# Moving the second layer's eight VectorE modulation slots into the first feed-forward, as sixteen half slots

## The chip, the cores and the metric

One Trainium2 chip, one core of it. The metric is the device time of one execution in microseconds (us); the kernel before takes 1564.17 us, the median of three runs.

## What is computed

A first block (a gMLP and RWKV mixer, then a mixture of 32 experts) and a second block of two transformer layers, over 256 tokens of width 1024, all in float32. Only the second block matters here. Cut to that:

```python
def second_block(x, c, w_mod, b_mod, ...):
    c_act = jax.nn.silu(c)                                          # (1, 1024)
    for i in range(2):
        mod = jnp.einsum('bd,dm->bm', c_act, w_mod[i]) + b_mod[i]   # (1, 6144)
        sh_a, sc_a, gt_a, sh_f, sc_f, gt_f = jnp.split(mod, 6, axis=-1)
        h = modulate(rmsnorm(x, g_mix_pre[i]), sh_a, sc_a)
        qkv = jnp.einsum('bsd,de->bse', h, w_qkv[i])
        ...                                                         # attention, 16 heads
        x = x + gt_a[:, None, :] * rmsnorm(o, g_mix_post[i])
        h = modulate(rmsnorm(x, g_ffn_pre[i]), sh_f, sc_f)
        gate = jnp.einsum('bsd,df->bsf', h, w_ffn_gate[i])          # f: 2816
        up = jnp.einsum('bsd,df->bsf', h, w_ffn_up[i])
        gate = causal_depthwise_conv(gate, w_conv[i], b_conv[i])    # width 3
        y = jnp.einsum('bsf,fd->bsd', jax.nn.silu(gate) * up, w_ffn_down[i])
        x = x + gt_f[:, None, :] * rmsnorm(y, g_ffn_post[i])
```

The vector `mod` of layer 1 depends on `c` and `w_mod[1]` alone, so it can be computed at any time before it is used. (Layers are counted from 0 in the code: layer 1 is the second.)

## The kernel before

Each engine runs its own program, and semaphores tie them. SyncE (SP) issues all weight loads on one DMA queue, in program order. Most go to `ring`, six slots of 2 MB, in turn; SP waits on `slot_freed` before it loads into a used slot, and TensorE on `slot{s}_loaded` before it reads one.

**Modulation.** `w_mod` of a layer is 1024 x 6144. Its 6144 columns are three groups of 2048 (group 0: `sh_a`, `sc_a`; group 1: `gt_a`, `sh_f`; group 2: `sc_f`, `gt_f`). A unit is 256 rows of one group, 2 MB, so a group has four units. Units are computed in one of two ways. On TensorE, `mod_slice` multiplies a unit in a ring slot by a column of SiLU(c), `silc`, into bank 0 of PSUM, `part`. On VectorE (DVE), a unit is a slot: `mod_slots` takes its two halves of 128 rows (1 MB each, tiles `mslots` in the arena), multiplies each by one column of `silc` and adds it into `macc2` (line 1892 for the first half of a group, line 1894 for all others), each step giving `mod_step`. TensorE then adds the 128 partitions of `macc2` into `part` with a column of ones (`add_slots`, line 1129). From there ScalarE (ACT) copies `part` to SBUF (`part_copy`), TensorE turns it into columns (`flush`, line 579) and DVE adds the bias into `modc` (`mod_columns`, line 1465).

Layer 1's group 0 is done by TensorE during layer 0. Its groups 1 and 2 are the eight slots of this case. SP loads them between the `w_qkv1` matrices (line 386), two slot buffers in turn, each load waiting for the `mod_step` that frees its buffer; the very first also waits for the end of the layer before (`x4_ready`). DVE works them off during layer 1's projections, and TensorE has `add_slots` and `flush` between projection units: after unit 4 the sum of group 1, after unit 8 the sum of group 2, and flushes after units 5 and 9. Units 0 to 7 are Q and K (line 1164), 8 and 9 are half of V (line 1182); the next work of TensorE is the scores of the attention (lines 1219 and 1220 in layer 0, 1224 in layer 1), which waits for ACT's copies of V (line 2306). `add_slots` waits for the `mod_step` count, and everything of TensorE stands behind it, since an engine runs in order.

**Feed-forward.** 22 tiles of 128 of the 2816 columns, in five ring groups of four tiles and a last one of two. A group is three loads: gate, up and down matrices, 2 MB each (line 430, `ffn_group`). For tile f TensorE runs `gate_up` (32 matmuls, line 1349, into bank 5 + f % 2); DVE runs `conv` (lines 2043, 2046, 2049), ACT the SiLU (line 2383), DVE `gated` (line 2054, gives `act_f`); and TensorE runs `down` of tile f (8 matmuls, line 1362), which waits for `act_f`. The order on TensorE is gate_up(f + 1), down(f), gate_up(f + 2), down(f + 1) and so on:

```python
gate_up(cur, 0, f)
down(prev, 3, f - 1, last_of=(0, 1, 3))     # frees the three slots of the group before
gate_up(cur, 1, f + 1)
down(cur, 0, f)
```

The three loads of group g + 1 wait for slots that group g - 1 frees in down(4g - 1), that is, right behind gate_up(4g).

Of the kernel before, what the change touches and what calls it, by code (L numbers as in the profile page):

```python
# [111 lines left out]
def build_program(nc, a):  # L112
    with ExitStack() as ctx:
# [128 lines left out]
        gmixb, gffnb = at(12288, D), at(13312, D)  # L242
        macc2 = at(10240, 2 * D)
        mslots = ((at(8192, 2 * D), at(12288, 2 * D)), (at(15360, 2 * D), at(17408, 2 * D)))
        diagd = at(14336, DC, P)
        t1 = at(15360, 2, 2, 384)
        sp_ = at(16896, 2, 2, 384)
# [30 lines left out]
        def _(sp):  # L278
# [82 lines left out]
            for layer in range(2):  # L361
                if layer == 0:
                    for i in range(4, 6):
                        load_mod("w_mod0", i)
                def qkv(i):

                    load(w_cols(a[f"w_qkv{layer}"], 512 * i), 4096)

                def w_o(i):

                    load(w_cols(a[f"w_o{layer}"], 512 * i), 4096)

                def mod_slot(j):

                    if j >= 2:
                        sp.wait_ge(S("mod_step"), 16 * layer + 2 * (j - 1))
                    elif layer == 1:
                        sp.wait_ge(S("x4_ready"), 2)
# [4 lines left out]
                    u = (18, 28)[layer] + j - 12  # L383
# [10 lines left out]
                mod_slot(0)  # L394
                mod_slot(1)
                if layer == 0:
                    qkv(2)
                mod_slot(2)
                mod_slot(3)
                qkv(3)  # L400
                mod_slot(4)
                mod_slot(5)
                qkv(4)
                mod_slot(6)
                mod_slot(7)
                qkv(5)
# [12 lines left out]
                wg, wu, wd = (a[f"w_ffn_{k}{layer}"] for k in ("gate", "up", "down"))  # L419


                def ffn_group(g, w, n, i):

                    wide = bass.ds(g * 512, w)
                    for k, src in enumerate((wg[:, wide].rearrange("(c p) n -> p c n", p=P),
                                             wu[:, wide].rearrange("(c p) n -> p c n", p=P),
                                             wd[wide, :].rearrange("(c p) n -> p c n", p=P))):
                        s = (n + k) % RING
                        sp.wait_ge(S("slot_freed"), i * RING + (n + k - RING + 1))
                        sp.dma_start(ring[:, s, 0:8 * w].rearrange("p (c n) -> p c n", c=src.shape[1]), src)\  # L430
                            .then_inc(S(f"slot{s}_loaded"), 16)

                ffn_group(0, 512, n0, 0)
                with sp.Fori(0, 2, 1) as i:
                    for k in range(2):
                        ffn_group(i * 2 + (1 + k), 512, n0 + 3 + 3 * k, i)
                ffn_group(5, 256, n0 + 15, 0)
                st_sp.n += 18
            for t in range(NT):
# [98 lines left out]
        def _(pe):  # L538
# [581 lines left out]
                    mod_slice(filled[0], silc)  # L1120
                    filled[0] += 1

            def add_slots(steps, start=True, stop=True):

                pe.wait_ge(S("mod_step"), steps)
                if start:
                    pe.wait_ge(S("mod_copied"), filled[0] // 4)
                for g in range(4):
                    last = mm(part[32 * g:32 * g + 1, :], ones[:, 0:1], macc2[:, 512 * g:512 * g + 512], start=start, stop=stop,
                              tile_position=(0, 32 * g))  # L1130
                if stop:
                    last.then_inc(S("part_done"), 1)

            def between_units(layer, u):

                if layer == 0 and u == 2:
                    add_slots(4, start=False)
                    filled[0] += 2
                if layer == 0 and u == 7:
                    add_slots(12)  # L1140
                    filled[0] += 4
                if layer == 1 and u in (4, 8):
                    add_slots(16 + 2 * u)
                    filled[0] += 4
                if u in ((3, 8), (5, 9))[layer]:
                    flush()

            fill1(2)
            for layer in range(2):
# [251 lines left out]
                        for k in range(3)]  # L1401
                g5 = group_slots(n0 + 15, 0, 256)
                gate_up(g5, 0, F0 + 20)
                down(prev, 3, F0 + 19, last_of=(0, 1), ts=(0,))
                gate_up(g5, 1, F0 + 21)
                down(prev, 3, F0 + 19, last_of=(3,), ts=(1,))
# [1 line left out]
                down(g5, 1, F0 + 21, final=True, ts=(0,), late=1)  # L1408
                down(g5, 0, F0 + 20, ts=(1,), late=1)
                down(g5, 1, F0 + 21, final=True, ts=(1,), late=1)  # L1410
                st_pe.n += 18
                ahead[0] = True

# [5 lines left out]
        def _(dve):  # L1419
# [461 lines left out]
            final_norm(1)  # L1881
            scaled_second(4)

            def mod_slots(layer, j0, j1, first):

                for j in range(j0, j1):
                    c0 = 2 * (((18, 28)[layer] + j) % 4)
                    dve.wait_ge(S(f"slot{6 + j % 2}_loaded"), 128 + 32 * (4 * layer + j // 2 + 1))
# [8 lines left out]
            for layer in range(2):  # L1897
# [1 line left out]
                evac_h(hTd, lm, 0, 8 + 8 * layer)  # L1899
                dve.wait_ge(S("turned"), 12 + 8 * layer)  # L1900
                if layer == 0:
                    mod_slots(0, 0, 2, True)
                    dve.wait_ge(S("part_done"), 5)
                    mod_slots(0, 2, 6, True)
                    mod_columns()
                    dve.wait_ge(S("part_done"), 6)
                    mod_slots(0, 6, 8, True)
                    mod_columns()
                else:
                    mod_slots(1, 0, 1, True)  # L1910

                    dve.wait_ge(S("fg_done"), 1)
                    H_ = slice(0, NH2)
# [6 lines left out]
                    dve.wait_ge(S("neg_made"), 3)  # L1920
                    d(V.tensor_tensor_scan(out=cum3[H_, P:384], data0=keep1, data1=v_, initial=0.0, op0=ALU.mult, op1=ALU.add))
                    d.to(V.tensor_copy(cum3[H_, 0:P], cum3[H_, P:2 * P]), "cum_ready")
                    mod_slots(1, 1, 4, False)
                    dve.wait_ge(S("part_done"), 8)
                    mod_slots(1, 4, 8, True)
                    mod_columns()
                    mod_columns()

                def post_diag(nm, dst):
# [127 lines left out]
                with dve.Fori(0, NFT // 2 - 1, 1) as i:  # L2057
                    for r in range(2):
                        conv(i * 2 + r, r)
                        gated(i * 2 + r, r)  # L2060
                for r in range(2):
                    conv(NFT - 2 + r, r)
                    gated(NFT - 2 + r, r, 1)
                dve.wait_ge(S("rows_copied"), 8 + 4 * layer)
                if layer == 0:
                    mod_columns()
                    gain_ready(2, 8, col("g_mix_pre", 8, 8))
                for t in range(NT):
                    for n in range(2):
# [8 lines left out]
        def _(act):  # L2078
# [205 lines left out]
            for layer in range(2):  # L2284
# [3 lines left out]
                for u in range(4):  # L2288
                    act.wait_ge(S("qk_done"), 8 * layer + 1 + u)
                    a_.to(A(QT[:, 2 * u:2 * u + 2, :], bank[1 + u].rearrange("p (m t) -> p m t", m=2), ACT.Copy,  # L2290
                      scale=HD ** -0.5), "q_copied")
                    if layer == 0 and u == 2:
                        part_copy()
                    if layer == 1 and u == 1:
                        H_ = slice(0, NH2)
# [3 lines left out]
                for u in range(4):  # L2299
                    act.wait_ge(S("qk_done"), 8 * layer + 5 + u)  # L2300
                    a_.to(A(KT[:, 2 * u:2 * u + 2, :], bank[1 + (4 + u) % 6].rearrange("p (m t) -> p m t", m=2), ACT.Copy), "k_copied")
                    if (layer, u) in ((0, 3), (1, 0)):
                        part_copy()
                for u in range(2):
                    act.wait_ge(S("v_done"), 4 * layer + 1 + u)
                    a_.to(A(Vd[:, u, 0:512], bank[1 + (8 + u) % 6][:, :], ACT.Copy), "v_copied")
                    if layer == 1 and u == 0:
                        part_copy()
                A8 = 8 * layer

                def log_term(m):
# [68 lines left out]
                with act.Fori(0, NFT // 2, 1) as i:  # L2380
                    for r in range(2):
                        act.wait_ge(S("conv_done"), i * 2 + (F0 + r + 1))
                        A(sv[:, r, :], cv[:, r, :], ACT.Silu).then_inc(S("silu_f"), 1)  # L2383
                nc.scalar.preload_act_table_set("natural_log_exp_and_others")
                for t in range(NT):
                    y_half(t, 0, 4 + 8 * layer)
# [77 lines left out]
```

## Time and profile before

| | |
|---|---|
| three runs | 1560.15, 1564.17, 1565.51 us |
| median | 1564.17 us |
| span of the profiled execution | 1562.6 us |
| TensorE busy | 1474.9 us, 94% of the span |
| VectorE busy | 463.8 us, 30% |
| ScalarE busy | 233.9 us, 15% |
| DMA over the span | 256 GB/s, 400.81 MB |

The span runs from the first to the last recorded instruction of the profiled execution; no other time of that execution is given. Its span lies 1.6 us below the median of the runs, which themselves lie 5.4 us apart. Times in views are us from the start of the span. In the stretch of the change the first feed-forward runs from 925.9 to about 1154, the second layer's projections from 1162.5 to 1245.0, and the second feed-forward from 1326.7 on.

### The profile page before, as it was taken

The page shows a single profiled execution, that of the slowest core. Times are in us where ns is not written, and L with a number is a line of the kernel's source. Part 1 is how long each engine was busy: PE and PEld are TensorE (multiplying, and loading weights), DVE is VectorE, ACT ScalarE, POOL GpSimd, SP SyncE. Part 2 cuts the span into 40 slices and gives each one's busy share as a digit, 9 for nine tenths or more (in the row PEclk, how much of TensorE's full clock was granted, in tenths as well). Part 3 has the DMA queues.
Part 4 walks back from the last instruction along what each step waited for, and adds up shares of the span by engine and source line. Part 5 has one row for each costly group of instructions (what it writes and reads, how often), then busy time and mean ns, then how long its engine had stood idle before and what let it go on. Part 6 is the DMA issues. An engine that isn't in the chain of part 4 may idle for free.

```text
span 1562.6 us, 21450 instructions
## 1 busy us (share of the span) xinstructions
PE 1474.9 (94%) x8392; PEld 946.4 (61%) x8393; DVE 463.8 (30%) x835; ACT 233.9 (15%) x469; POOL 22.0 (1%) x69
## 2 busy tenths in 40 slices
PE   5999999999989999999799999999989998999998
PEld 2866774544444444444485657777768564777775
DVE  1355545311111111111544321111145472111112
ACT  1230002200000000000313430000031062100001
POOL 2000000000000000000000000000000000000000
PEclk7999999999999999999999999999999999999999
DMA  9665524899999999999998150344276923144420
GB/s 376 226 247 216 217 109 170 344 424 421 423 385 399 425 428 426 425 428 424 407 405 323 51 219 22 142 160 161 81 285 249 395 93 108 54 162 161 161 81 27
DMA packets 89961, 400.81 MB, mean 256 GB/s; under 512 B 7040, under 2 KB 12288, under 8 KB 63264
## 3 DMA queue, kind: packets, MB, share of 16 engines
q1 hardware_dynamic: 89888, 399.73, 64.4%
q8 instruction: 59, 0.97, 0.2%
q14 instruction: 14, 0.11, 0.0%
HBM read 398.66 MB, written 1.05 MB: 256 GB/s over the span
## 4 chain that ended last, share of the span: by engine, by line
PE 75%; DMA 10%; DVE 7%; issue 3%; DVEq 3%; ACT 1%; SPq 0%; ACTq 0%
PE psum L1349 20%; PE psum L1019 12%; PE psum L1362 10%; DMA ring<-in_moe_up 7%; PE psum L1164 5%; PE psum L629 4%; PE psum L1312 4%; PE psum L1007 2%; DMA arena<-in_w_mod 2%; PE psum L752 2%; PE psum L566 2%; PE psum L1197 2%; PE psum L1182 1%; DMA ring<-in_ada_w 1%; DVE arena L1894 1%
## 5 line engine op out<-in xcount | busy, mean ns | idle before, releaser
L1019 PE MATMUL psum<-ring,arena 128*64 128x256 f32 (+1 forms) x2240 | 306.8, 428 | 20.8 <-DMA ring<-in_moe_up 8.7
L1349 PE MATMUL psum<-arena,ring 128*128 128x256 f32 x1408 | 313.3, 381 | 0.1
L1349 PEld LDWEIGHTS psum<-arena,ring 128*128 128x128 f32 x1408 | 268.8, 191 | 54.5 <-issue 19.5
L1019 PEld LDWEIGHTS psum<-ring,arena 128*64 128x64 f32 x2240 | 161.7, 138 | 174.3 <-issue 80.2
L1362 PE MATMUL psum<-ring,arena 128*128 128x512 f32 x352 | 157.9, 592 | 0.0
L2043 DVE TENSOR_SCALAR arena<-psum,cols 128x256 f32<-128x256 f32 x44 | 24.0, 544 | 325.5 <-PE psum L1349 325.5
L1164 PE MATMUL psum<-arena,ring 128*128 128x256 f32 x512 | 113.5, 383 | 0.2
L1164 PEld LDWEIGHTS psum<-arena,ring 128*128 128x128 f32 x512 | 97.8, 192 | 16.0 <-issue 2.7
L1362 PEld LDWEIGHTS psum<-ring,arena 128*128 128x128 f32 x352 | 66.9, 190 | 66.3 <-issue 63.6
L1807 DVE TENSOR_TENSOR arena<-psum,arena 128x256 f32<-128x256 f32 x32 | 13.6, 425 | 254.8 <-PE psum L1019 254.8
L2383 ACT ACTIVATE arena<-arena 128x256 f32<-128x256 f32 x44 | 18.3, 417 | 417.8 <-DVE arena L2049 417.8
L1007 PE MATMUL psum<-arena 64*128 64x512 f32 x272 | 76.2, 639 | 2.1 <-ACTq L2237 1.4
L1894 DVE SCALAR_TENSOR_TENSOR arena<-arena,small 128x2048 f32<-128x2048 f32 x27 | 63.5, 2352 | 17.6 <-DMA arena<-in_w_mod 16.7
L2246 ACT ACTIVATE arena<-psum 128x512 f32<-128x512 f32 x32 | 19.1, 597 | 305.4 <-PE psum L1019 305.4
L629 PE MATMUL psum<-arena,ring 128*128 128x256 f32 x256 | 56.4, 380 | 0.0
L1312 PE MATMUL psum<-ring,arena 128*128 128x512 f32 x128 | 55.5, 594 | 0.9 <-DVE arena L1940 0.9
L629 PEld LDWEIGHTS psum<-arena,ring 128*128 128x128 f32 x256 | 48.5, 190 | 8.1 <-issue 1.6
L1019 PE MATMUL psum<-arena 128*64 128x256 f32 (+1 forms) x320 | 43.1, 424 | 0.8 <-DVE arena L1803 0.8
L1312 PEld LDWEIGHTS psum<-ring,arena 128*128 128x128 f32 x128 | 24.2, 190 | 31.7 <-issue 30.5
L1803 DVE COPY arena<-arena 128x512 f32 x32 | 13.7, 427 | 96.5 <-issue 86.0
L1019 PEld LDWEIGHTS psum<-arena 128*64 128x64 f32 x320 | 22.3, 137 | 22.9 <-issue 9.9
L752 PE MATMUL psum<-arena 64*64 64x64 f32 x896 | 30.5, 220 | 4.4 <-DVE arena L1634 2.6
(381 smaller groups left out, 1214.4 us busy)
## 6 DMA issues: line engine op xcount, KB each, us to landing
ring<-in_moe_gate SPq DMA_DIRECT2D x28, 2048.0 KB, 19.6
ring<-in_moe_up SPq DMA_DIRECT2D x28, 2048.0 KB, 18.0
ring<-in_moe_down SPq DMA_DIRECT2D x28, 2048.0 KB, 18.6
arena<-in_w_mod SPq DMA_DIRECT2D x32, 1024.0 KB, 9.8
ring<-in_ada_w SPq DMA_DIRECT2D x12, 2048.0 KB, 10.4
ring<-in_w_qkv SPq DMA_DIRECT2D x12, 2048.0 KB, 15.0
ring<-in_w_ffn_gate SPq DMA_DIRECT2D x10, 2048.0 KB, 7.7
ring<-in_w_ffn_up SPq DMA_DIRECT2D x10, 2048.0 KB, 12.4
```

The costliest lines, as they stand in the source:

```text
L566: last = mm(part[32 * g:32 * g + 1, :], vec[:, c:c + 1], w[:, cc, 512 * g:512 * g + 512], start=(c == 0), stop=(c == DC - 1), tile_positio ...
L629: last = mm(b[:, mi * TOK:(mi + 1) * TOK], w[:, c, m * P:(m + 1) * P], hT[:, c, :], start=(c == 0), stop=(c == DC - 1))
L752: last = mm(out[ps, j * CH:(j + 1) * CH], left(ps, j), right(ps, j), start=True, stop=True, tile_position=(ps.start, ps.start))
L1007: last = mm(bank[4 + 2 * t + n][:, :], pwin[hs, t * P:(t + 1) * P], ym[hs, :], start=first, stop=(name is not None), skip_group_check=True)
L1019: ins = mm(bank[b][o, 0:n], lhsT, w[:, half * n:(half + 1) * n], start=first, stop=last, tile_position=(0, 64 * half))
L1164: last = mm(bank[1 + u % 6][:, mi * TOK:(mi + 1) * TOK], w[:, c, m * P:(m + 1) * P], hTd[:, c, :], start=(c == 0), stop=(c == DC - 1))
L1197: last = mm(bank[0][:, t * TOK:(t + 1) * TOK], hTd[:, c, t * P:(t + 1) * P], w_late[:, c, TOK * b:TOK * b + TOK], start=(c == 0), stop=(c ...
L1312: last = mm(bank[1 + 2 * t + n][:, :], oT[:, c, t * P:(t + 1) * P], w[n][:, c, :], start=(c == 0), stop=(c == DC - 1))
L1349: last = mm(b[:, k * TOK:(k + 1) * TOK], sl[k][2][:, c, j * P:(j + 1) * P], hTd[:, c, :], start=(c == 0), stop=(c == DC - 1))
L1362: ins = mm(bank[1 + 2 * t + n][:, :], actF[:, late, j % 2, t * P:(t + 1) * P], sl[2][2][:, j, n * 512:(n + 1) * 512], start=first, stop=fi ...
L1894: ins = V.scalar_tensor_tensor(out=macc2, in0=w, scalar=by, in1=macc2, op0=ALU.mult, op1=ALU.add)
L2043: V.tensor_scalar(c, z[:, 0:TOK], w(2), cols[:, bass.ds(f + cb, 1)], ALU.mult, ALU.add)\
```

## The change

Groups 1 and 2 of layer 1's modulation leave the projections of layer 1. They become sixteen half slots of 1 MB (`late_half`), worked off by DVE in layer 0's feed-forward, one behind `gated` of each of tiles 0 to 15. Halves 0 to 7 sum into `late_sum[0]` (group 1), halves 8 to 15 into `late_sum[1]` (group 2). SP issues their loads four at a time, behind the three loads of ring groups 1 to 4: halves 4g - 4 to 4g - 1 behind ring group g. There are two buffers, `late_w`; the load of half h waits until DVE is through with half h - 2. TensorE adds `late_sum[0]` in the last ring group of layer 0's feed-forward and flushes behind its last `down`; it adds `late_sum[1]` after unit 1 of layer 1's projections and flushes after unit 4. ACT's copies follow. The `mod_columns` of group 0 moves from the end of the feed-forward to tile 2. For layer 0 the loops over feed-forward tiles are written out on DVE and SP.

```diff
+        late_w = (at(2048, 2 * D), at(4096, 2 * D))
+        late_sum = (at(6144, 2 * D), at(8192, 2 * D))
@@ SyncE, projections
                 if layer == 1:
+                    for i in range(2, 6):
+                        qkv(i)
+                else:
+                    mod_slot(0)
+                    mod_slot(1)
                     qkv(2)
...
@@ SyncE, feed-forward
+                def late_half(h):
+                    if h < 2:
+                        sp.wait_ge(S("o_done"), 8)
+                    else:
+                        sp.wait_ge(S("mod_step"), 16 + h - 1)
+                    g, r = divmod(4 + h // 2, 4)
+                    sp.dma_start(late_w[h % 2], a["w_mod1"][256 * r + P * (h % 2):256 * r + P * (h % 2) + P,
+                                                            2048 * g:2048 * g + 2048]).then_inc(S(f"slot{6 + h % 2}_loaded"), 16)
                 ffn_group(0, 512, n0, 0)
+                if layer == 0:
+                    for g in range(1, 5):
+                        ffn_group(g, 512, n0 + 3 * g, 0)
+                        for h in range(4 * g - 4, 4 * g):
+                            late_half(h)
@@ TensorE, projections
-                if layer == 1 and u in (4, 8):
-                    add_slots(16 + 2 * u)
+                if layer == 1 and u == 1:
+                    add_slots(32, sums=late_sum[1])
                     filled[0] += 4
-                if u in ((3, 8), (5, 9))[layer]:
+                if u in ((3, 8), (4,))[layer]:
                     flush()
@@ TensorE, feed-forward
                 gate_up(g5, 0, F0 + 20)
+                if layer == 0:
+                    add_slots(24, sums=late_sum[0])
+                    filled[0] += 4
...
                 down(g5, 1, F0 + 21, final=True, ts=(1,), late=1)
+                if layer == 0:
+                    flush()
@@ VectorE
+            def late_half(h):
+                dve.wait_ge(S(f"slot{6 + h % 2}_loaded"), 256 + 16 * (h // 2 + 1))
+                to, by = late_sum[h // 8], silc[:, h % 8:h % 8 + 1]
+                if h % 8 == 0:
+                    ins = V.tensor_scalar(to, late_w[h % 2], by, None, ALU.mult)
+                else:
+                    ins = V.scalar_tensor_tensor(out=to, in0=late_w[h % 2], scalar=by, in1=to, op0=ALU.mult, op1=ALU.add)
+                d.to(ins, "mod_step")
...
-                    mod_slots(1, 0, 1, True)
+                    mod_columns()
...
-                    mod_slots(1, 1, 4, False)
-                    dve.wait_ge(S("part_done"), 8)
-                    mod_slots(1, 4, 8, True)
-                    mod_columns()
                     mod_columns()
...
+                if layer == 0:
+                    for f in range(NFT - 2):
+                        conv(f, f % 2)
+                        gated(f, f % 2)
+                        if f == 2:
+                            mod_columns()
+                        if f < 16:
+                            late_half(f)
...
                 if layer == 0:
-                    mod_columns()
                     gain_ready(2, 8, col("g_mix_pre", 8, 8))
@@ ScalarE
-                    if layer == 0 and u == 2:
+                    if u == 2:
                         part_copy()
-                    if (layer, u) in ((0, 3), (1, 0)):
+                    if (layer, u) == (0, 3):
                         part_copy()
-                    if layer == 1 and u == 0:
-                        part_copy()
...
+                if layer == 0:
+                    part_copy()
                 nc.scalar.preload_act_table_set("natural_log_exp_and_others")
```

## Rows read from the trace of the kernel before

**Rows 1.** Page, busy time by engine: us, share of the span, instructions.
```profile
PE 1474.9 (94%) x8392; PEld 946.4 (61%) x8393; DVE 463.8 (30%) x835; ACT 233.9 (15%) x469; POOL 22.0 (1%) x69
```

**Rows 2.** TensorE's timeline, layer 1's projections: start us, us, engine, line, operation, count, [idle before].
```profile
1201.71 1.04 PE L1129 MATMUL psum<-arena,ones 128*1 128x512 f32 x8 [0.35 <-DVE arena L1894]
...
1224.40 7.03 PE L1182 MATMUL psum<-ring,arena 128*128 128x512 f32 x16
1234.15 1.04 PE L1129 MATMUL psum<-arena,ones 128*1 128x512 f32 x8 [2.72 <-DVE modc L1465]
1235.12 8.83 PE L1182 MATMUL psum<-ring,arena 128*128 128x512 f32 x16
1243.79 0.95 PE L579 MATMUL psum<-ident,macc 128*128 128x4 f32 x8
1245.01 0.49 PE L1224 MATMUL psum<-arena 64*128 64x128 f32 x4 [0.27 <-issue]
```

**Rows 3.** VectorE's timeline in the same stretch.
```profile
1207.34 1.29 DVE L1892 TENSOR_SCALAR arena<-arena,small 128x2048 f32<-128x2048 f32 x1 [5.68 <-DMA arena<-in_w_mod]
...
1229.06 4.74 DVE L1894 SCALAR_TENSOR_TENSOR arena<-arena,small 128x2048 f32<-128x2048 f32 x2 [0.24 <-DMA arena<-in_w_mod]
```

**Rows 4.** Windows of 1 us: PE, PEld, DVE, ACT, POOL busy, PEclk granted, DMA share, GB/s.
```profile
1163.00:1164.00 1.00, 1.00 (x4) 0.79 (x4) 0.55 (x1) 0.97 (x2) 0.00 (x0) 0.62 1.02 434
...
1236.00:1237.00 1.00, 1.00 (x3) 0.48 (x2) 0.00 (x0) 0.00 (x0) 0.00 (x0) 0.50 1.06 389
...
1239.00:1240.00 1.00, 1.00 (x4) 0.45 (x3) 0.00 (x0) 0.00 (x0) 0.00 (x0) 1.00 1.06 391
```

**Rows 5.** TensorE's timeline, layer 0, the first scores behind V.
```profile
841.34 0.71 PE L1219 MATMUL psum<-arena 64*128 64x256 f32 x4 [0.95 <-ACT arena L2306]
```

**Rows 6.** TensorE's timeline, layer 0's feed-forward, tiles 4 to 7.
```profile
971.76 3.60 PE L1362 MATMUL psum<-ring,arena 128*128 128x512 f32 x8
...
992.44 3.60 PE L1362 MATMUL psum<-ring,arena 128*128 128x512 f32 x8
995.87 7.07 PE L1349 MATMUL psum<-arena,ring 128*128 128x256 f32 x32
```

**Rows 7.** VectorE's timeline, layer 0's feed-forward, tile 4: first and last step.
```profile
972.19 0.54 DVE L2043 TENSOR_SCALAR arena<-psum,cols 128x256 f32<-128x256 f32 x1 [7.64 <-PE psum L1349]
...
974.47 0.42 DVE L2054 TENSOR_TENSOR arena<-arena,psum 128x256 f32<-128x256 f32 x1 [0.48 <-ACT arena L2383]
```

**Rows 8.** SyncE's timeline and issues' time to landing (us, last column), ring group 2.
```profile
972.97 0.37 SPq L430 DMA_DIRECT2D ring<-in_w_ffn_gate  x1
...
975.53 1.55 SPq L430 DMA_DIRECT2D ring<-in_w_ffn_down  x1
...
ring<-in_w_ffn_gate SPq DMA_DIRECT2D x1, 2048.0 KB, 7.7
ring<-in_w_ffn_up SPq DMA_DIRECT2D x1, 2048.0 KB, 12.4
ring<-in_w_ffn_down SPq DMA_DIRECT2D x1, 2048.0 KB, 15.6
```

**Rows 9.** The same, a modulation slot behind a projection matrix, 1190 to 1196.
```profile
1190.42 0.43 SPq L284 DMA_DIRECT2D ring<-in_w_qkv  x1
1194.35 8.14 SPq L386 DMA_DIRECT2D arena<-in_w_mod  x4
...
ring<-in_w_qkv SPq DMA_DIRECT2D x1, 2048.0 KB, 11.8
...
arena<-in_w_mod SPq DMA_DIRECT2D x1, 1024.0 KB, 10.4
...
arena<-in_w_mod SPq DMA_DIRECT2D x1, 1024.0 KB, 12.5
```

**Rows 10.** Groups by line, 900 us on: count, busy us, mean ns, idle before.
```profile
L1894 DVE SCALAR_TENSOR_TENSOR arena<-arena,small 128x2048 f32<-128x2048 f32 x14 | 32.9, 2352 | 11.7 <-DMA arena<-in_w_mod 11.2 <-DVE arena L1922 0.2
```

**Rows 11.** TensorE's timeline, the first work of layer 1 behind layer 0.
```profile
1158.76 3.68 PE L1111 MATMUL psum<-ident,arena 128*128 128x128 f32 x16 [4.19 <-DVE arena L1863]
```

More of the change, by code:

```diff
@@ L375, in mod_slot @@
                     if j >= 2:
-                        sp.wait_ge(S("mod_step"), 16 * layer + 2 * (j - 1))
-                    elif layer == 1:
-                        sp.wait_ge(S("x4_ready"), 2)
+                        sp.wait_ge(S("mod_step"), 2 * (j - 1))
                     elif j == 0:
@@ L382, in mod_slot @@
                         sp.wait_ge(S("x2_sum"), 2)
-                    u = (18, 28)[layer] + j - 12
+                    u = 18 + j - 12
                     g, r = divmod(u % 12, 4)
@@ L392, in _ @@
                 if layer == 1:
-                    qkv(2)
[L394 to L406, printed above, removed]
+                    for i in range(2, 6):
[3 more added lines that the diff above has]
+                    mod_slot(1)
+                    qkv(2)
+                    mod_slot(2)
+                    mod_slot(3)
+                    qkv(3)
+                    mod_slot(4)
+                    mod_slot(5)
+                    qkv(4)
+                    mod_slot(6)
+                    mod_slot(7)
+                    qkv(5)
                 w_o(0)
@@ L431, in ffn_group @@
                             .then_inc(S(f"slot{s}_loaded"), 16)
-                ffn_group(0, 512, n0, 0)
-                with sp.Fori(0, 2, 1) as i:
-                    for k in range(2):
-                        ffn_group(i * 2 + (1 + k), 512, n0 + 3 + 3 * k, i)
+                def late_half(h):
[6 more added lines that the diff above has]
+                                                            2048 * g:2048 * g + 2048]).then_inc(S(f"slot{6 + h % 2}_loaded"), 16)
+                ffn_group(0, 512, n0, 0)
+                if layer == 0:
[4 more added lines that the diff above has]
+                else:
+                    with sp.Fori(0, 2, 1) as i:
+                        for k in range(2):
+                            ffn_group(i * 2 + (1 + k), 512, n0 + 3 + 3 * k, i)
                 ffn_group(5, 256, n0 + 15, 0)
@@ L1121, in fill1, with add_slots @@
                     filled[0] += 1
-            def add_slots(steps, start=True, stop=True):
+            def add_slots(steps, start=True, stop=True, sums=None):
                 pe.wait_ge(S("mod_step"), steps)
@@ L1128, in add_slots @@
                 for g in range(4):
-                    last = mm(part[32 * g:32 * g + 1, :], ones[:, 0:1], macc2[:, 512 * g:512 * g + 512], start=start, stop=stop,
+                    last = mm(part[32 * g:32 * g + 1, :], ones[:, 0:1], (macc2 if sums is None else sums)[:, 512 * g:512 * g + 512], start=start, stop=stop,
                               tile_position=(0, 32 * g))
@@ L1882, in _, with mod_slots @@
             scaled_second(4)
-            def mod_slots(layer, j0, j1, first):
+            def late_half(h):
[3 more added lines that the diff above has]
+                    ins = V.tensor_scalar(to, late_w[h % 2], by, None, ALU.mult)
+                else:
+                    ins = V.scalar_tensor_tensor(out=to, in0=late_w[h % 2], scalar=by, in1=to, op0=ALU.mult, op1=ALU.add)
+                d.to(ins, "mod_step")
+            def mod_slots(j0, j1, first):
                 for j in range(j0, j1):
-                    c0 = 2 * (((18, 28)[layer] + j) % 4)
-                    dve.wait_ge(S(f"slot{6 + j % 2}_loaded"), 128 + 32 * (4 * layer + j // 2 + 1))
+                    c0 = 2 * ((18 + j) % 4)
+                    dve.wait_ge(S(f"slot{6 + j % 2}_loaded"), 128 + 32 * (j // 2 + 1))
                     for h in range(2):
@@ L1901, in _ @@
                 if layer == 0:
[L1902 removed]
+                    mod_slots(0, 2, True)
                     dve.wait_ge(S("part_done"), 5)
[L1904 removed]
+                    mod_slots(2, 6, True)
                     mod_columns()
                     dve.wait_ge(S("part_done"), 6)
[L1907 removed]
+                    mod_slots(6, 8, True)
                     mod_columns()
                 else:
[L1910 removed]
+                    mod_columns()
                     dve.wait_ge(S("fg_done"), 1)
@@ L2055, in gated @@
                         .then_inc(S("act_f"), 1)
[L2057 to L2060, printed above, removed]
+                if layer == 0:
[6 more added lines that the diff above has]
+                            late_half(f)
+                else:
+                    with dve.Fori(0, NFT // 2 - 1, 1) as i:
+                        for r in range(2):
+                            conv(i * 2 + r, r)
+                            gated(i * 2 + r, r)
                 for r in range(2):
```

## The prediction

> **What bounds the kernel now.** I read the busy line first: TensorE is at work for 94% of the span and VectorE for 30% [rows 1], so a change to VectorE's work counts only where TensorE waits for it. Next the chain of waits through the second layer's projections, and then TensorE's timeline there, to see how long each of its waits is. There are two at `add_slots` [rows 2]: 0.35 us ahead of the sum at 1201.71 and 2.72 us ahead of that at 1234.15. VectorE's timeline says what is late: it stood 5.68 us without data for the first half of the second group, and its last two steps run from 1229.06 to 1233.80, past the end of TensorE's unit 8 (1224.40 + 7.03 = 1231.43) [rows 2, 3]. So in this stretch the slots' transfers, which share SyncE's queue with the projection matrices, set TensorE's wait. The granted clock shows what follows: at 1236 it is 0.50 (1.2 GHz), and 1.00 again only at 1239 [rows 4]. That is why 16 matmuls of V take 8.83 us, where the same 16 ahead of the wait took 7.03 [rows 2].
>
> In the first feed-forward nothing waits: TensorE repeats 10.34 us per tile ((992.44 - 971.76) / 2), 6.91 of gate_up and 3.43 of down [rows 6], and VectorE needs 974.89 - 972.19 = 2.70 us of each, having been idle for 7.64 [rows 7]. By busy time, a half slot of 2.35 us [rows 10] fits there three times over. What decides is when its data comes, so the last views are SyncE's timeline and the times to landing.
>
> **What the projections gain.** Wait and sum: from 1224.40 to 1235.12 TensorE needs 10.72 us for one half of V; without the wait and the sum it needs 6.9. Gain 3.8. Clock: with no idle ahead of it the next half takes 7.03 in place of 8.83. Gain 1.8. The wait of 0.35 goes, with the restart behind it: 0.4. The sum that stood there stays, since one is now taken behind unit 1, when all of its 16 steps have long been done. The flush behind unit 9 (0.95) moves under the idle time behind the feed-forward, but here it saved little: it stood where TensorE would otherwise wait for ScalarE's copy of V. Layer 0 has no flush there, and shows that wait, 0.95 us [rows 5]. From 1243.79 to 1245.01 are 1.22 now; I keep 1.0 of it. Gain 0.2. Together 6.2, bounds 5.4 (the copy costs as much as the flush, the clock gives back 1.2) and 6.6.
>
> **What the feed-forward pays on TensorE.** One sum of 1.04 [rows 2] in the last group, on the path: 1.0. The flush there lies in the 4.19 us in which TensorE waits for the first scaled x [rows 11]: nothing, and were that cover gone, 0.95. ScalarE's copy of `part` (0.6) and its table load fit ahead of the first square of the sum. `mod_columns` at tile 2 and the written-out loops fall into VectorE's 7.64 us of idle time: nothing.
>
> **When the half slots' data comes.** Let T be the end of gate_up(4k), 971.9 for tile 4. Right behind it TensorE frees the slots for the next ring group, and SyncE issues three loads of 2 MB at 972.97, 973.67 and 975.53. They land 7.7, 12.4 and 15.6 us after their issue [rows 8]: at 980.7, 986.1 and 991.1. The first took no longer for the two behind it, and each next one lands some 5 us later: the queue serves them one after another. Half 4 of the modulation is the next issue behind these three, at 977.1 or a little later; but tile 4 is done on VectorE at 974.9 [rows 7], and there the engine waits for it. A 1 MB half behind a 2 MB matrix can be seen too: the matrix issued at 1190.42 lands 11.8 later, at 1202.2; the half issued behind it, at 1194.35, lands 10.4 later, at 1204.8, or 2.6 behind the matrix; and its sister 2.5 behind that [rows 9] (VectorE starts on it at 1207.34 [rows 3]). So half 4 lands at 991.1 + 2.6 = 993.7, that is T + 21.8, and half 5 at T + 24.4.
>
> The Trainium skill, page "DMA: Bandwidth & Descriptors", section "Queues, rings and completion order", has each DMA engine consume descriptors in ring order, while warning that a later transfer may still complete before an earlier one. By ring order the sum here stands; by the warning alone half 4 could come a little sooner than 993.7, but not ahead of data that the engines have not yet started on.
>
> **The stall.** VectorE: half 4 from 993.8 to 996.1 (2.36), and only then conv and gated of tile 5, which are queued behind it: 2.70, to 998.9. TensorE wants down(5) at 992.44 [rows 6], and everything behind stands with it. Stall 6.4 us. Half 5 follows on VectorE from 998.9 to 1001.2 (its data came at 996.3), tile 6 is gated at 1004, and TensorE asks for it only at 998.9 + 3.4 + 6.9 = 1009.2: no second stall. Half 6 is issued at 996.1 on an empty queue and half 7 at 1001.2: no stall. So one stall for each ring group whose halves are issued behind a whole group's loads in time with its tiles: groups 2, 3 and 4, at down(5), down(9) and down(13). Half 8 is the first of a sum, the 1.29 us form [rows 3], so its stall is 5.4. Ring group 1 is loaded earlier; its last matrix was issued at 926.7, and halves 0 and 1, of 1 MB, should be there by about 944, while down(1) is wanted only at 951: none. Together 6.4 + 5.4 + 6.4 = 18.2, bounds 16.4 (each half lands 0.6 sooner) and 21.2 (1 us later).
>
> **Clock behind each stall.** No row shows an idle of 6.4 us in this stretch; the nearest are 2.72 us, which cost 1.8 (above), and 4.19 us [rows 11], behind which the granted clock is still 0.62 in the window of 1163 [rows 4]. TensorE had started again at 1158.76, so some 4.6 us ran at half clock: 2.3 lost. I take 2.3, being nearest to the longer idle: 3 x 2.3 = 6.9, bounds 5.4 and 9.
>
> **Sum.** -6.2 + 1.0 + 18.2 + 6.9 = +19.9 us. The profiled span is 1562.6, so its next would be 1582.5; the median of the runs is 1.6 above that span, and 1564.2 + 19.9 = 1584.1. Bounds of this case: 1578 (-6.6 + 1.0 + 16.4 + 5.4 = +16.2 less the 2 us by which runs scatter) to 1591 (-5.4 + 1 + 21.2 + 9 = +25.8 and rounding). About 0.3%, 4.7 us, is what a measurement can tell from no change.
>
> **Rivals.** (a) *No stall: faster.* If the halves shared the queue's rate with the matrices instead of waiting behind them, half 4 would be there when some 3 MB had moved since its issue, 7.7 us by the gate matrix's row, at 985. The point that decides: to have tile 5 gated by 992.44 the half must land by 992.44 - 2.70 - 2.36 - 0.1 = 987.3, 10.2 us after its issue. For it: halves among projection matrices landed 10.4 and 12.5 us after issue, not far off. Against it: those had one matrix ahead, these have two and a half, and their landings line up one behind another [rows 8, 9]. Time: 1564.2 - 6.2 + 1.0 = 1559.0. Chance 7%.
>
> (b) *Part of the stall.* The halves' long rows go faster than the matrices', or they overlap the tail of the last matrix by 3 us or so. Then stalls are 3.4, 2.4 and 3.4, and the clock costs 1.8 each as behind 2.72 us of idle: -5.2 + 9.2 + 5.4 = +9.4, 1573.6. Chance 8%.
>
> (c) *Stalls without a price in clock.* If the fall of the clock fell inside the stalls: -5.2 + 18.2 = +13, 1577. Against it: both idle times above were followed by a low clock. Chance 7%.
>
> (d) *The change doesn't give what it takes from the projections*, because something else is as late there (ScalarE's copies, the matrices). Then +26.1, 1590.3. Against it: without slots the queue there has less to carry, and in layer 0 the same units show no other wait than the 0.95. Chance 5%.
>
> **Chances and range.** The forecast holds 73%. The range 1571 to 1590 takes in (b), (c) and nearly all of the forecast's own, 1578 to 1591; outside lie (a), part of (d) and a tail. Faster by over 0.3% needs (a) and a little luck, since (a) is -5.2: 0.06. Within 0.3%: the rest of (a) and a very short stall: 0.04. Slower: 0.90.
>
> **What would show it.** In the changed profile TensorE should wait before line 1362 three times for over 5 us in the first feed-forward, the releaser being VectorE's gated, and VectorE should wait at the halves' lines for a transfer of `w_mod`, some 19 us at halves 4, 8 and 12 each; the granted clock should be 0.5 behind each wait. The projections from the first Q matmul to the first scores should take 82.5 - 6.2 = 76.3 us. The prediction is wrong if the halves land less than 10 us after their issue behind a ring group's loads, or if SyncE issues them ahead of these.

## The result, and the profile after

The changed kernel takes 1580.74 us (median of 6 runs, 1578.79 to 1591.73), the kernel before 1563.87 us (6 runs, 1560.15 to 1568.89). The ratio is 1.0114, with a 95% interval of 1.0088 to 1.0139: slower by 1.1%. Forecast were 1584 us, with a range of 1571 to 1590. The profiled execution took 1581.58 us with a span of 1579.5; so about 2 us lie around a span.

The busy line of the changed kernel's page hardly shows this: against [rows 1] TensorE has 5 us more and VectorE 1 us less.

```profile
PE 1480.1 (94%) x8392; PEld 947.0 (60%) x8393; DVE 462.7 (29%) x835; ACT 233.5 (15%) x469; POOL 22.0 (1%) x69
```

The groups by line do. Here is `down`, before (line 1362) and now (line 1379); it had no idle time ahead of it and has 17.0 us:

```profile
L1362 PE MATMUL psum<-ring,arena 128*128 128x512 f32 x352 | 157.9, 592 | 0.0
...
L1379 PE MATMUL psum<-ring,arena 128*128 128x512 f32 x352 | 165.3, 615 | 17.0 <-DVE arena L2082 17.0
```

TensorE's timeline in the first feed-forward, for tiles 4 to 7 (compare [rows 6]) and then the two later places; in brackets the idle time ahead of the row and its releaser:

```profile
983.43 7.07 PE L1366 MATMUL psum<-arena,ring 128*128 128x256 f32 x32
996.48 6.24 PE L1379 MATMUL psum<-ring,arena 128*128 128x512 f32 x8 [5.98 <-DVE arena L2082]
1002.56 7.07 PE L1366 MATMUL psum<-arena,ring 128*128 128x256 f32 x32
...
1033.58 7.07 PE L1366 MATMUL psum<-arena,ring 128*128 128x256 f32 x32
1045.71 5.40 PE L1379 MATMUL psum<-ring,arena 128*128 128x512 f32 x8 [5.05 <-DVE arena L2082]
1050.94 7.07 PE L1366 MATMUL psum<-arena,ring 128*128 128x256 f32 x32
...
1081.96 7.07 PE L1366 MATMUL psum<-arena,ring 128*128 128x256 f32 x32
1095.04 6.46 PE L1379 MATMUL psum<-ring,arena 128*128 128x512 f32 x8 [6.01 <-DVE arena L2082]
1101.33 7.07 PE L1366 MATMUL psum<-arena,ring 128*128 128x256 f32 x32
```

Three waits, ahead of down(5), down(9) and down(13), each for `gated`. Start to start, a gate_up takes 6.91 us, so the waits are 996.48 - 983.43 - 6.91 = 6.14, then 5.22 and 6.17 us: 17.5 together. Behind each, the eight matmuls that need 3.43 us from start to start need 6.08, 5.23 and 6.29: 7.3 us more. VectorE's timeline names the cause, tile 4 and half 4 (compare [rows 7]), and the first half of the next group:

```profile
972.02 0.42 DVE L2082 TENSOR_TENSOR arena<-arena,psum 128x256 f32<-128x256 f32 x1 [0.48 <-ACT arena L2417]
991.56 2.35 DVE L1913 SCALAR_TENSOR_TENSOR arena<-arena,small 128x2048 f32<-128x2048 f32 x1 [19.11 <-DMA arena<-in_w_mod]
993.95 0.54 DVE L2071 TENSOR_SCALAR arena<-psum,cols 128x256 f32<-128x256 f32 x1
...
996.01 0.42 DVE L2082 TENSOR_TENSOR arena<-arena,psum 128x256 f32<-128x256 f32 x1 [0.48 <-ACT arena L2417]
...
1041.85 1.29 DVE L1911 TENSOR_SCALAR arena<-arena,small 128x2048 f32<-128x2048 f32 x1 [19.25 <-DMA arena<-in_w_mod]
```

VectorE is through with tile 4 at 972.4, waits 19.11 us for a transfer, and only then takes up tile 5, whose gate_up ended near 980. SyncE's timeline and the time to landing of the issues there (last column) say why the transfer is late (compare [rows 8]):

```profile
970.71 0.38 SPq L431 DMA_DIRECT2D ring<-in_w_ffn_gate  x1
971.57 0.38 SPq L431 DMA_DIRECT2D ring<-in_w_ffn_up  x1
973.28 0.37 SPq L431 DMA_DIRECT2D ring<-in_w_ffn_down  x1
973.70 25.35 SPq L441 DMA_DIRECT2D arena<-in_w_mod  x4
...
ring<-in_w_ffn_down SPq DMA_DIRECT2D x1, 2048.0 KB, 15.8
arena<-in_w_mod SPq DMA_DIRECT2D x1, 1024.0 KB, 17.8
```

The last matrix lands at 973.28 + 15.8 = 989.1, half 4 at 973.70 + 17.8 = 991.5, 2.4 us behind. The windows of the first wait, with the granted clock in the column after POOL, show the second price:

```profile
992.00:994.00 2.00, 0.00 (x0) 0.00 (x0) 1.96 (x2) 0.00 (x0) 0.00 (x0) 1.00 0.61 254
...
997.00:998.00 1.00, 1.00 (x2) 0.34 (x1) 1.00 (x1) 0.00 (x0) 0.00 (x0) 0.50 0.99 418
...
1001.00:1002.00 1.00, 1.00 (x3) 0.44 (x2) 1.00 (x2) 0.00 (x0) 0.00 (x0) 0.68 1.05 442
1002.00:1003.00 1.00, 1.00 (x5) 0.57 (x4) 1.00 (x1) 0.00 (x0) 0.00 (x0) 1.00 0.80 336
```

TensorE stands from 990.5. The clock is 1.00 (2.4 GHz) up to 994, falls to 0.50 (1.2 GHz) during the wait and is back to 1.00 only at 1002, some 5 us after the work went on. At down(9) it fell later, only when TensorE was at work again:

```profile
1045.00:1046.00 1.00, 0.29 (x1) 0.29 (x2) 0.77 (x2) 0.20 (x1) 0.00 (x0) 1.00 0.83 344
1046.00:1047.00 1.00, 1.00 (x2) 0.34 (x2) 1.00 (x1) 0.00 (x0) 0.00 (x0) 0.50 1.00 426
```

There it is back at about 1049.4, and the eight matmuls lose 1.80 us where those of down(5) lose 2.65.

In the second layer's projections the two sums are no longer waited for (compare [rows 2]). What is left is a wait of 1.05 us for ScalarE's copy of V, ahead of the first scores:

```profile
1247.25 13.90 PE L1199 MATMUL psum<-ring,arena 128*128 128x512 f32 x32
1262.20 0.49 PE L1241 MATMUL psum<-arena 64*128 64x128 f32 x4 [1.05 <-ACT arena L2342]
...
1263.90 3.27 PE L1214 MATMUL psum<-ring,arena 128*128 128x256 f32 x8
```

Both halves of V take 13.90 us together, as against 7.03 and 8.83 with a wait of 2.72 and a sum between them.

Stretch by stretch, from the first matmul of one part to the first of the next (us):

| kernel | ahead of the first feed-forward | feed-forward and turn to layer 1 | projections | attention | `w_o` and turn | first two gate_ups | rest |
|---|---|---|---|---|---|---|---|
| before | 925.9 | 236.7 | 82.5 | 46.8 | 34.9 | 16.0 | 220.0 |
| changed | 923.8 | 262.7 | 75.8 | 48.1 | 34.9 | 14.4 | 219.9 |
| difference | -2.1 | +26.0 | -6.7 | +1.3 | 0.0 | -1.5 | 0.0 |

The sum is +16.9 us, as the spans have it (1579.5 - 1562.6).

### The profile page after: what moved, and what is told of

Read it like the earlier page. It is cut to its first block, busy times and chain, and to the rows that moved or that the text cites. A ratio compares the mean times of both kernels' runs of the same rounds, so it can differ in the third digit from the quotient of the medians.

```text
span 1579.5 us, 21244 instructions
## 1 busy us (share of the span) xinstructions
PE 1480.1 (94%) x8392; PEld 947.0 (60%) x8393; DVE 462.7 (29%) x835; ACT 233.5 (15%) x469; POOL 22.0 (1%) x69
## 3 DMA queue, kind: packets, MB, share of 16 engines
HBM read 398.66 MB, written 1.05 MB: 253 GB/s over the span
## 4 chain that ended last, share of the span: by engine, by line
PE 73%; DMA 13%; DVE 6%; DVEq 3%; issue 3%; ACT 1%; SPq 0%; ACTq 0%
PE psum L1366 17%; PE psum L1036 11%; PE psum L1379 9%; DMA ring<-in_moe_up 8%; PE psum L1181 7%; PE psum L646 4%; PE psum L1329 4%; DMA arena<-in_w_mod 3%; PE psum L1024 2%; PE psum L1199 2%; PE psum L769 2%; PE psum L1214 2%; PE psum L583 1%; DMA ring<-in_ada_w 1%; DVE arena L1833 1%
## 5 line engine op out<-in xcount | busy, mean ns | idle before, releaser
L1036 PE MATMUL psum<-ring,arena 128*64 128x256 f32 (+1 forms) x2240 | 304.5, 425 | 18.6 <-DMA ring<-in_moe_up 12.2
L1379 PE MATMUL psum<-ring,arena 128*128 128x512 f32 x352 | 165.3, 615 | 17.0 <-DVE arena L2082 17.0
L1329 PE MATMUL psum<-ring,arena 128*128 128x512 f32 x128 | 55.5, 594 | 0.6 <-DVE arena L1968 0.6
L1913 DVE SCALAR_TENSOR_TENSOR arena<-arena,small 128x2048 f32<-128x2048 f32 x14 | 32.9, 2347 | 38.3 <-DMA arena<-in_w_mod 38.3
## 6 DMA issues: line engine op xcount, KB each, us to landing
ring<-in_w_ffn_up SPq DMA_DIRECT2D x10, 2048.0 KB, 12.4
```

Of the source, the lines that this page charges most:

```text
L1036: ins = mm(bank[b][o, 0:n], lhsT, w[:, half * n:(half + 1) * n], start=first, stop=last, tile_position=(0, 64 * half))
L1329: last = mm(bank[1 + 2 * t + n][:, :], oT[:, c, t * P:(t + 1) * P], w[n][:, c, :], start=(c == 0), stop=(c == DC - 1))
L1379: ins = mm(bank[1 + 2 * t + n][:, :], actF[:, late, j % 2, t * P:(t + 1) * P], sl[2][2][:, j, n * 512:(n + 1) * 512], start=first, stop=fi ...
L1913: ins = V.scalar_tensor_tensor(out=to, in0=late_w[h % 2], scalar=by, in1=to, op0=ALU.mult, op1=ALU.add)
```

## The experiments

The theory to test has four links: the halves wait in one queue behind 6 MB; VectorE waits for them with the next tile behind it; TensorE waits for that tile; and then it works at half clock. All times below go with their own runs of the kernel before. These had a median of 1566.44 us for four of the kernels (halves two further ahead, halves one tile later, no loads, 13 fillers) and 1565.34 for the other three, so ratios are compared, not times. The runs of one kernel lie 7 to 20 us apart, and in the profiled ones the part ahead of the first feed-forward alone lies between 923.1 and 931.6 us. The stretch of the feed-forward, read from one profiled execution of each kernel, does not depend on it, and carries the verdicts.

**Halves issued two further ahead.** The same work in another order on SyncE.

```diff
-                        for h in range(4 * g - 4, 4 * g):
+                        for h in range((0, 6, 10, 14)[g - 1], (6, 10, 14, 16)[g - 1]):
                             late_half(h)
```

> The changed kernel with the half slots issued two further ahead: halves 0 to 5 behind ring group 1, 6 to 9 behind group 2, 10 to 13 behind group 3, 14 and 15 behind group 4. The same work on every engine. Theory (the half waits in the queue behind its own ring group's 6 MB, and VectorE waits for it with the next tile's conv behind it): half 6 is still issued behind group 2's loads and lands about 22 us after gate_up(4), but VectorE wants it only at 20.7 + 2.4 = 23.1 us; no wait before down(5), (9) and (13), no low clock behind them. Time 1580.7 - 17.5 - 7.3 = about 1556. Rival (VectorE's 2.35 us steps, or traffic of the halves beside the matrices, slow the tiles whatever the order): waits of about 6 us stay, time about 1580.

Measured: 1560.99 us, ratio 0.9959 (0.9928 to 0.9989), where 1556 to 1563.87 is 0.995. The feed-forward's stretch is 237.8 us, in place of 262.7. Its VectorE timeline at tile 6:

```profile
998.48 0.54 DVE L2071 TENSOR_SCALAR arena<-psum,cols 128x256 f32<-128x256 f32 x1 [5.59 <-PE psum L1366]
...
1000.88 2.35 DVE L1913 SCALAR_TENSOR_TENSOR arena<-arena,small 128x2048 f32<-128x2048 f32 x1
```

VectorE waits for TensorE now (5.59 us), and takes half 6 with no wait, though that was still issued behind a ring group's 6 MB. The same sixteen steps and transfers cost TensorE nothing here. Compared to before, the stretch is 1.2 us longer, of which 1.0 is the sum that moved there.

**VectorE's halves one tile later.** SyncE as in the changed kernel.

```diff
-                        if f < 16:
-                            late_half(f)
+                        if 1 <= f < 17:
+                            late_half(f - 1)
```

> The changed kernel with VectorE's halves one tile later: half f behind gated of tile f + 1. SyncE's order and the moment at which the halves land stay as they are. Theory (not the late landing costs, but that conv and gated of the next tile stand behind VectorE's wait for it): half 4 is waited for behind gated(5), from about 13 to 22 us after gate_up(4), while tile 6 comes at 20.7 and its down is wanted at 31; no wait of TensorE. About 1556. Rival (the transfers themselves disturb TensorE's reads or the matrices' landing): waits before down(5), (9) and (13) stay, about 1580.

Measured: 1561.4 us, ratio 0.9953 (0.9927 to 0.9978), stretch 237.6 us. VectorE's timeline at half 4, and TensorE's at down(6) and its neighbours:

```profile
985.90 0.42 DVE L2082 TENSOR_TENSOR arena<-arena,psum 128x256 f32<-128x256 f32 x1 [0.48 <-ACT arena L2417]
994.99 2.35 DVE L1913 SCALAR_TENSOR_TENSOR arena<-arena,small 128x2048 f32<-128x2048 f32 x1 [8.67 <-DMA arena<-in_w_mod]
997.38 0.54 DVE L2071 TENSOR_SCALAR arena<-psum,cols 128x256 f32<-128x256 f32 x1
```

```profile
986.97 7.07 PE L1366 MATMUL psum<-arena,ring 128*128 128x256 f32 x32
993.87 3.60 PE L1379 MATMUL psum<-ring,arena 128*128 128x512 f32 x8
997.31 7.07 PE L1366 MATMUL psum<-arena,ring 128*128 128x256 f32 x32
1004.21 3.60 PE L1379 MATMUL psum<-ring,arena 128*128 128x512 f32 x8
```

The half is as late as before and VectorE still waits 8.67 us for it, but tile 5 is already done and tile 6 is taken up 7 us before its down. TensorE's timeline has no gap. So not the lateness of the half costs, but what stands behind the wait.

**No loads.** VectorE's sixteen steps stay, the loads of halves 2 to 15 go. The modulation vector of layer 1 is then computed from wrong weights in its groups 1 and 2.

```diff
                 def late_half(h):
+                    if h >= 2:
+                        return
...
-                dve.wait_ge(S(f"slot{6 + h % 2}_loaded"), 256 + 16 * (h // 2 + 1))
+                dve.wait_ge(S(f"slot{6 + h % 2}_loaded"), 256 + 16)
```

> The changed kernel without the loads of halves 2 to 15: VectorE does all sixteen steps at their places, on the contents of the two buffers that halves 0 and 1 were loaded into, so the modulation vector of layer 1 (groups 1 and 2) is computed from wrong weights. Theory: all of the loss in the feed-forward comes from waiting for the loads; VectorE's own steps fit into its idle time: about 1556, TensorE's period 10.34 us for every tile. Rival (VectorE's steps cost by themselves): a few us above 1556, with waits at the tiles that have a step.

Measured: 1558.58 us, ratio 0.9954 (0.9934 to 0.9974), stretch 237.6 us, no wait of TensorE in it for VectorE's tiles. VectorE's steps cost nothing, and leaving the transfers out is worth no more than moving them by two. The matrices of the ring groups, with no halves behind them, land hardly sooner for it: 7.6 (gate), 12.2 (up) and 15.5 us (down) after issue in ring group 2, and 7.8, 12.4 and 15.8 in the changed kernel.

**One more megabyte ahead.** A load that nobody reads, ahead of the halves of ring groups 2 to 4.

```diff
+                        if g > 1:
+                            sp.wait_ge(S("lora_in"), 32 + 16 * (g - 2))
+                            sp.dma_start(idle_w, a["w_mod1"][0:P, 0:2048]).then_inc(S("lora_in"), 16)
                         for h in range(4 * g - 4, 4 * g):
                             late_half(h)
```

> The changed kernel with one more load of 1 MB, of data that nobody reads, issued between the loads of ring groups 2, 3 and 4 and their half slots. Theory (one queue, served in order): halves 4, 8 and 12 land 2.5 us later, each of the three waits of TensorE grows by 2.5 us to 8.6, 7.7 and 8.7 us, time 1580.7 + 7.5 = about 1588. Rival (the waits come from a fixed cost at the ring group's change, or transfers share the rate): the waits stay at 6.1, 5.2 and 6.2 us, or grow by less than 1 us; time within 3 us of 1580.7.

Measured: 1592.11 us, ratio 1.0192 (1.0157 to 1.0226). TensorE's timeline at the three places:

```profile
983.43 7.07 PE L1370 MATMUL psum<-arena,ring 128*128 128x256 f32 x32
998.75 6.33 PE L1383 MATMUL psum<-ring,arena 128*128 128x512 f32 x8 [8.24 <-DVE arena L2086]
...
1050.31 6.15 PE L1383 MATMUL psum<-ring,arena 128*128 128x512 f32 x8 [7.31 <-DVE arena L2086]
...
1102.63 5.59 PE L1383 MATMUL psum<-ring,arena 128*128 128x512 f32 x8 [8.25 <-DVE arena L2086]
```

The waits are 2.26, 2.26 and 2.24 us longer than in the changed kernel, 6.8 in all, and the stretch is 269.4 in place of 262.7: 6.7 more. The extra megabyte costs each wait some 2.25 us; the forecast of 2.5 was a little high. The restarts at low clock did not get dearer with the longer waits. Whom the extra load delayed tells more than by how much, since transfers that shared the rate could also make a later one wait longer. Here are the times to landing in ring group 2, of the last matrix and of the extra load (issued at 973.70):

```profile
ring<-in_w_ffn_down SPq DMA_DIRECT2D x1, 2048.0 KB, 15.5
arena<-in_w_mod SPq DMA_DIRECT2D x1, 1024.0 KB, 17.6
```

The matrix ahead of it lands no later than without it (15.8), the extra load lands at 991.3, and half 4 behind it is taken up at 993.82, where it was 991.56. So here a load is delayed by what stands ahead of it in the queue, and not by what stands behind.

The whole time rose by more than the stretch: the ratio went from 1.0114 to 1.0192, some 12 us, while the profiled execution, the fastest of its four, has a span only 6.0 us longer. The intervals leave room for 6.7 us; whether there is more, and where, no profile shows.

**Matmuls in the wait.** Fillers whose results are not used go ahead of down(5), (9) and (13), and TensorE's loop is written out for layer 0.

```diff
                     gate_up(cur, 2, f + 2)
+                    if layer == 0 and f < 16:
+                        pe.wait_ge(S("mod_copied"), filled[0] // 4)
+                        for _ in range(11 if f == 8 else 13):
+                            mm(bank[0][:, :], ones[:, :], hTd[:, 0:2, :], start=True, stop=True)
                     down(cur, 1, f + 1)
```

> The changed kernel with 13, 11 and 13 matmuls of 512 columns into the free bank 0 ahead of down(5), down(9) and down(13) of layer 0; their results are not used. (TensorE's loop over ring groups is written out for layer 0.) They take about 0.43 us each, 5.6, 4.7 and 5.6 us, and so lie inside the waits of 6.1, 5.2 and 6.2 us. Theory (the wait costs twice: itself, and half clock behind it): waits of about 0.5 us are left, down(5), (9) and (13) take 3.6 us in place of 6.2, 5.4 and 6.5: 7.3 us less, about 1573.5. Rival (these down matmuls are slow for another cause, such as VectorE and DMA at the same memory): they stay slow, and the time stays about 1580.7.

Measured: 1589.79 us, ratio 1.0146 (1.0113 to 1.0178): slower still. The fillers were twice as long as I had reckoned:

```profile
989.71 11.32 PE L1410 MATMUL psum<-arena,ones 128*128 128x512 f32 x26
1000.86 3.60 PE L1379 MATMUL psum<-ring,arena 128*128 128x512 f32 x8
```

Thirteen calls are 26 matmuls in the record: each of these float32 matmuls shows as two. They outlast the wait by 5 us. But down(5) takes 3.60 us behind them, where it took 6.24. So the same experiment again, with 6, 5 and 6 fillers:

```diff
-                        for _ in range(11 if f == 8 else 13):
+                        for _ in range(5 if f == 8 else 6):
```

> The run before with fewer fillers. There one filler of 512 columns showed as two matmuls of 0.43 us, so the 13 fillers took 11.2 us, outlasted the wait by 5 us, and the time rose; but down(5), (9) and (13) behind them took 3.60 us. Now 6, 5 and 6 fillers, 5.2, 4.3 and 5.2 us, inside waits of 6.1, 5.2 and 6.2 us; their results are not used. Theory (half clock follows from the wait): waits of about 0.9 us are left, the downs behind take 3.6 us, and the feed-forward is 7.3 us shorter than in the changed kernel: about 1573.5. Rival (the clock falls for another cause, or a wait of 0.9 us is enough for it): the downs stay at 5.4 to 6.5 us, time about 1580.7.

Measured: 1582.04 us, ratio 1.0118 (1.0059 to 1.0178), an interval too wide to tell it from the changed kernel. The stretch can: 257.9 us in place of 262.7. TensorE's timeline:

```profile
992.91 5.31 PE L1410 MATMUL psum<-arena,ones 128*128 128x512 f32 x12
998.89 3.70 PE L1379 MATMUL psum<-ring,arena 128*128 128x512 f32 x8 [0.67 <-DVE arena L2093]
...
1045.24 3.70 PE L1379 MATMUL psum<-ring,arena 128*128 128x512 f32 x8 [0.43 <-DVE arena L2093]
...
1093.93 5.40 PE L1379 MATMUL psum<-ring,arena 128*128 128x512 f32 x8 [1.92 <-DVE arena L2093]
```

At the first two places the waits that are left are short and the downs full speed. At the third the half landed later in this execution and 1.92 us were left idle; the clock was still 1.00 in the window of 1094, when TensorE worked again, and 0.50 in that of 1096. So the low clock follows from TensorE's idle time, as stated. The forecast 7.3 us back became 4.7. The first two places gave 2.7 and 2.0. The third gave nothing: its down lost 1.8 us in place of 2.9, but TensorE waited 1.1 us longer for it (7.2 from the end of gate_up, fillers included, in place of 6.2).

**The flush behind unit 9.** On top of the halves issued ahead: the flush at its old place in the projections.

```diff
-                if u in ((3, 8), (4,))[layer]:
+                if u in ((3, 8), (9,))[layer]:
                     flush()
```

> The kernel with the half slots issued two further ahead, and with the one flush of layer 1's projections behind unit 9, where the kernel before had it, in place of behind unit 4. Theory (behind V TensorE waits 1.05 us for ScalarE's copy, and the clock falls there: the 8 matmuls of late V behind it take 3.3 us in place of 2.0): the flush lies in that wait, the clock stays, and 0.8 + 1.6 = 2.4 us are won against the same kernel with the flush behind unit 4: ratio 0.9943 to the kernel before. Rival (the low clock there has another cause): only the 0.8 us, and the matmuls of late V stay slow.

Measured: 1557.12 us, ratio 0.9948 (0.9920 to 0.9976). The projections take 74.9 us in place of 75.8, so the flush is indeed free behind V:

```profile
1234.84 0.95 PE L596 MATMUL psum<-ident,macc 128*128 128x4 f32 x8
1236.05 0.49 PE L1241 MATMUL psum<-arena 64*128 64x128 f32 x4 [0.27 <-issue]
```

On the clock it says less. Late V takes 1.99 us here, but the attention's stretch is 46.5 us also in four kernels that keep the wait for ScalarE's copy (halves a tile later, no loads, one more megabyte, 6 fillers), and 48.1 to 48.2 in the other three (changed, two ahead, 13 fillers). Where the clock fell, it did so some 2 us after TensorE was at work again (in the changed kernel it is 1.00 in the window of 1263 and 0.50 in that of 1265). So behind a wait of 1.05 us the clock fell in three executions and not in four; whether the wait is the cause, and whether the flush prevents it, one profile of each kernel can't settle. The ratio is the lowest here, 0.5% under the kernel before; its interval overlaps with those of the two reordered ones.

| kernel | ratio to before | feed-forward | projections | attention |
|---|---|---|---|---|
| changed | 1.0114 | 262.7 | 75.8 | 48.1 |
| two ahead | 0.9959 | 237.8 | 75.8 | 48.2 |
| a tile later | 0.9953 | 237.6 | 75.9 | 46.5 |
| no loads | 0.9954 | 237.6 | 75.9 | 46.5 |
| 1 MB more ahead | 1.0192 | 269.4 | 76.8 | 46.5 |
| 13, 11, 13 fillers | 1.0146 | 269.6 | 75.8 | 48.1 |
| 6, 5, 6 fillers | 1.0118 | 257.9 | 75.8 | 46.5 |
| two ahead, flush behind V | 0.9948 | 237.7 | 74.9 | 46.5 |

The 76.8 in the projections of the kernel with 1 MB more is low clock again: behind the turn to layer 1 it lasted until 1195, 2 us into the first 64 matmuls of Q, which took 15.0 us in place of 14.0.

## Why the prediction was right

**The projections' gain** was forecast as 6.2 us and is 6.7. Both halves of V now take 13.9, as reckoned. The wait for ScalarE's copy that appears once the flush is gone was read from layer 0 as 0.95 [rows 5], and is 1.05. The rest of the difference is the first 64 matmuls of Q, which took 0.5 us less in this execution: the low clock behind the turn had ended before them (1.00 from 1186 on), where in the kernel before it reached 1.2 us into them [rows 4]. The reckoning had no such term.

**The landing.** Half 4 was put 2.6 us behind the last matrix, and landed 2.4 behind. That one queue serves the loads in order was a reading of two places in the trace, and the Trainium skill's page "DMA: Bandwidth & Descriptors", section "Queues, rings and completion order", has each DMA engine take descriptors in ring order. The extra megabyte agrees with both: 2.25 us for 1 MB, at each of three places, and no delay for the matrix ahead of it. The same section warns that a later transfer may complete first; in the ring group read here none did.

**The stalls** were forecast as 6.4, 5.4 and 6.4 (18.2) at down(5), (9) and (13), and are 6.1, 5.2 and 6.2 (17.5), at these places and no other. Most of the 0.2 to 0.3 us each is VectorE's chain, which takes 2.5 us with its loop written out, from 993.95 to 996.43, where it took 2.70 in the loop [rows 7]. The two reordered kernels show that the queueing of VectorE's next tile behind the wait is the necessary link.

**The clock** was taken as 2.3 us for each, from idle times shorter than the ones to come, and is 2.65, 1.80 and 2.86: 7.3 in place of 6.9. The fillers show that it hangs on the idle time. The single prices depend on how much of the low clock falls behind the restart (down(5) and down(9) above); that their sum comes out within 0.4 is in part luck.

**The sum in the last ring group** cost the 1.0 us forecast: the undisturbed stretches are 0.9 to 1.2 us longer than before.

The stretch comes to 26.0 us more, where 18.2 + 6.9 + 1.0 = 26.1 were forecast. The whole was forecast as +19.9 and is +16.9. Of the 3.0 us, 2.1 lie ahead of the first feed-forward, where the change has no part, and 0.5 in the projections. Two more places were not in the sum and nearly cancel, which is luck: +1.3 in the attention, where the clock was 0.50 in the window of 1265 and the kernel before had 1.00 from 1243 to 1250, and -1.5 in the second feed-forward's first tiles, where it was low until about 1346.4, 1.2 us into them, and before until 1331, 4.3 us into them. Rival (a) needed half 4 to land about 10 us after its issue; it took 17.8. Rival (b) wanted the half 3 us sooner, and it came within 0.2 of the forecast; (c) and (d) are refuted by the times of the downs behind the waits and of the projections.

## What to carry to other kernels

Idle time of an engine is room for moved work only if the work's data is there: read from the queue when its transfer can land, behind everything issued ahead of it, and then look at what the engine has queued behind its wait. Here an engine with work for less than half of each tile (2.5 us, and 2.35 of the moved step, in 10.34) stalled the bound one three times, and issuing the same loads two steps earlier, or taking each up a step later, turned a loss of 1.1% into a gain of 0.4 to 0.5%. And a wait of TensorE of 5 us or more was to be counted with the low clock behind it, here 40% on top.

## What was not expected of the hardware

Short idle times can matter too: TensorE's clock fell behind a wait of 1.92 us and cost 1.8 us there. It also fell behind one of 1.05 to 1.08 us in three of seven profiled executions, at a price of 1.6 us; that the wait is the cause there is not shown. In these four places the clock was still 1.00 when TensorE went back to work, and fell 1.2 to 2.3 us later. Behind 0.43 and 0.67 us it stayed. The price did not grow with the wait either: behind waits of 7.5 and 8.4 us the eight matmuls took 5.6 to 6.3 us, behind 5.2 to 6.2 us they took 5.4 to 6.5.
